# Stationary activation tiles 1088, 1056 and 1040 bytes apart instead of 1024

## The chip, the core and the metric

The kernel runs on one core of one Trainium2 chip. The metric is the device time of one execution in microseconds. Three executions of the kernel before took 1676.47, 1676.90 and 1677.61 us; their median, 1676.9 us, is what the change is measured against.

## What is computed

One decoder layer on 256 tokens with a model width of 2048, all in float32. The parts that matter here are its large matrix products, since nearly all of the time is theirs:

```python
h = _rms_norm(x, attn_norm_g[l])
proj = h @ w_in[l]                      # 2048 x 13312
...
kv = m @ w_mem_kv                       # 2048 x 2048, m is the normalised memory
...
merged = (jax.nn.sigmoid(g_da) * (o_da @ w_o_da[l])
          + jax.nn.sigmoid(g_ret) * (o_ret @ w_o_ret[l])
          + jax.nn.sigmoid(g_mem) * (o_mem @ w_o_mem[l]))
x = x + merged @ w_out[l]
hf = _rms_norm(x, ffn_norm_g[l])
x = x + (jax.nn.silu(hf @ w_ffn_gate[l]) * (hf @ w_ffn_up[l])) @ w_ffn_down[l]   # 2048 x 5632 twice, 5632 x 2048
```

Between them stand a causal differential attention, a chunked retention and a cross-attention into 256 memory tokens, which are small.

## The kernel before

**Operands.** The weights are streamed from HBM in pieces of 256 rows by 512 columns (512 KB each), 584 of them, into a ring of four slots named `raw`. ScalarE copies a piece into `w_hi`, which rounds it to the type float32r (L337, and L374 for the first four), and VectorE writes the rest, `raw - w_hi`, into `w_lo` (L625, L658). The activations are kept transposed, so that they can be the stationary operand: 16 tiles of 128 rows (of the contracted dimension) by 256 tokens, again in a high and a low part. `hT_hi` and `hT_lo` hold the normalised input of the projections, of the gates and of the feed-forward; `oT_hi` and `oT_lo` hold the memory at first, then the outputs of the branches, the merged rows, and the feed-forward's activations. These are the four sets of the title. In each the token is the fastest index, so one tile fills 256 x 4 = 1024 bytes of every partition, and the tiles follow each other without a gap.

**The product.** `three_passes` (L1007) issues three matmuls of 128 x 128 by 128 x 512 for one tile k, one half t of the tokens and one piece: high by high, high by low, low by high. The stationary operand is half a tile, 128 elements or 512 bytes of each partition; the moving operand is one row block of the piece, 512 elements or 2048 bytes of each partition. `pair` (L1014) does that for two tiles and two halves, twelve matmuls on one piece of weights, after a wait on `lo_done`. `chunk_pair` (L1024) puts eight such pairs (four or two where the contracted dimension is shorter) into one accumulation. Each matmul is an instruction for the weight load (named PEld in the profile) and one for the product (PE).

**Order.** Every engine runs a program written out by hand. The slots s of a sweep are the same on all engines: between its pieces TensorE does the small transposes (L1032) and the small products of the attentions (L1070, L1085, L1119 to L1137, L1160 to L1173) in float32. The stages are the memory's key and value, the projections, three gate and branch stages, the output projection, and eleven rounds of the feed-forward, each of 16 pieces of gate and up and 8 of down. In the feed-forward TensorE turns the activations after slot 2, ScalarE and VectorE write the first four tiles of `oT_hi` and `oT_lo` in one instruction each at slot 3 (L585, L957), and TensorE reads them from slot 16 on.

**Memory.** `sb(name, shape, type)` takes the next bytes of each partition. In the order of the calls `raw`, `w_hi` and `w_lo` take 16384 bytes each, then the four sets 16384 bytes each, then `proj` and the rest. Counted from the start of `raw`, the sets begin at 49152, 65536, 81920 and 98304 and `proj` at 114688, all multiples of 1024.

Of the kernel before, what the change touches and what calls it, by code (L numbers as in the profile page):

```python
# [27 lines left out]
F32R = mybir.dt.float32r  # L28
# [5 lines left out]
P = 128  # L34
D = 2048
TB = 2
TOK = TB * P
NCOL = 512
KD = D // P
# [37 lines left out]
def program(nc, x, mem, positions, w_in, da_q_norm_g, da_k_norm_g, da_lambda_q1, da_lambda_k1,  # L77
# [6 lines left out]
    with ExitStack() as ctx:  # L84
        def sb(name, shape, dt=F32):
            return ctx.enter_context(nc.sbuf_tensor(name, shape, dt))
# [5 lines left out]
        raw = sb("raw", [P, RING, 2, NCOL])  # L92
        w_hi = sb("w_hi", [P, RING, 2, NCOL], F32R)
        w_lo = sb("w_lo", [P, RING, 2, NCOL], F32R)
        hT_hi = sb("hT_hi", [P, KD, TOK], F32R)
        hT_lo = sb("hT_lo", [P, KD, TOK], F32R)
        oT_hi = sb("oT_hi", [P, KD, TOK], F32R)
        oT_lo = sb("oT_lo", [P, KD, TOK], F32R)
        proj = sb("proj", [P, TB, GATE0])
        kvm = sb("kvm", [P, TB, D])  # L100
        sq = sb("sq", [P, TB, 2, 256])
# [1177 lines left out]
```

## Time and profile before

| | |
|---|---|
| median of three timed executions | 1676.9 us (1676.47 to 1677.61) |
| span of the profiled execution, first to last instruction | 1674.9 us |
| the median less that span | 2.0 us |
| TensorE products (PE) busy | 1668.0 us, 7592 instructions |
| weight loads (PEld) busy | 1381.3 us, 7592 instructions |
| VectorE (DVE), ScalarE (ACT), GpSimd (POOL) busy | 950.0, 774.7, 31.9 us |
| moved by DMA | 319.96 MB, mean 191 GB/s |

The span is from the trace of one execution; the time of an execution holds about 2 us around it. Matmuls are pipelined: the profile gives each 128 x 512 product about 0.39 us, but one starts every 0.23 us, so that busy time of PE says only that the engine was never empty. What a matmul costs is read from the distance between the starts, or from the length of a stretch of the chain divided by its count. The chain is the sequence of work that ended last, followed back from the end.

### The profile page before, as it was taken

The numbers are of one execution on the slowest core, as the hardware profiler recorded it, in microseconds if no ns is written. First come the engines' busy times: TensorE is split into PE (matmuls) and PEld (weight loads), VectorE is DVE, ScalarE is ACT, GpSimd is POOL, SyncE is SP. The second block draws the span as 40 slices with busy tenths as digits, with TensorE's granted clock in tenths as the row PEclk, the third lists the DMA queues.
The fourth block names the chain that finished last, engine by engine and source line by source line (L and its number), as shares of the span: only waits on it lengthen the run. The fifth ranks groups of instructions, "written<-read, shape, count | busy, mean of one in ns | idle before, by whom it ended". The sixth has DMA issues, their size and how long they took to land.

```text
span 1674.9 us, 21891 instructions
## 1 busy us (share of the span) xinstructions
PE 1668.0 (100%) x7592; PEld 1381.3 (82%) x7592; DVE 950.0 (57%) x1061; ACT 774.7 (46%) x936; POOL 31.9 (2%) x33
## 2 busy tenths in 40 slices
PE   9999999999999999999999999999999999999999
PEld 7888888888888888888888888888888888888887
DVE  5565554454577766655555545565554554655555
ACT  6655454444555544444444544444434444444342
POOL 0000000000111000000000000000000000000000
PEclk9999999999999999999999999999999999999999
DMA  9876555566544565666655666666666666666664
GB/s 340 265 217 187 176 169 168 177 196 192 174 152 150 180 185 175 213 199 190 188 184 184 186 189 192 191 193 188 188 192 190 190 192 188 189 192 191 192 189 151
DMA packets 167095, 319.96 MB, mean 191 GB/s; under 512 B 11152, under 2 KB 15760, under 8 KB 166288
## 3 DMA queue, kind: packets, MB, share of 16 engines
q1 hardware_dynamic: 167056, 319.45, 62.1%
q8 instruction: 24, 0.39, 0.1%
q14 instruction: 15, 0.12, 0.0%
HBM read 317.31 MB, written 2.10 MB: 191 GB/s over the span
## 4 chain that ended last, share of the span: by engine, by line
PE 91%; issue 7%; DVE 1%; DMA 0%; POOL 0%; ACT 0%; DVEq 0%; ACTq 0%; SPq 0%; POOLq 0%
PE acc L1010 87%; PE at L1032 2%; POOL rstd L315 0%; PE at L1070 0%; PE at L1085 0%; DMA raw<-in_w_mem_kv 0%; DVE w_lo L625 0%; DMA raw<-in_w_in 0%; ACT pm L486 0%; PE at L1160 0%; DVE ss L650 0%; ACT w_hi L337 0%; PE at L1172 0%; PE at L1173 0%; PE at L1171 0%
## 5 line engine op out<-in xcount | busy, mean ns | idle before, releaser
L625 DVE TENSOR_TENSOR w_lo<-raw,w_hi 128x1024 fp32r<-128x1024 f32 x580 | 706.7, 1224 | 639.5 <-ACT w_hi L337 637.6
L337 ACT ACTIVATE w_hi<-raw 128x1024 fp32r<-128x1024 f32 x580 | 614.6, 1061 | 829.4 <-PE acc L1010 812.7
L1010 PE MATMUL acc<-w_hi,hT_hi 128*128 128x512 f32 x1568 | 616.7, 393 | 0.0
L1010 PE MATMUL acc<-w_hi,hT_lo 128*128 128x512 f32 x1568 | 611.0, 390 | 0.0
L1010 PE MATMUL acc<-w_lo,hT_hi 128*128 128x512 f32 x1568 | 610.5, 389 | 0.0
L1010 PEld LDWEIGHTS acc<-w_hi,hT_hi 128*128 128x128 f32 x1568 | 294.5, 188 | 62.2 <-issue 1.3
L1010 PEld LDWEIGHTS acc<-w_hi,hT_lo 128*128 128x128 f32 x1568 | 294.4, 188 | 61.9
L1010 PEld LDWEIGHTS acc<-w_lo,hT_hi 128*128 128x128 f32 x1568 | 294.6, 188 | 59.8
L1010 PE MATMUL acc<-w_hi,oT_hi 128*128 128x512 f32 x768 | 300.9, 392 | 1.2 <-DVE oT_lo L644 1.2
L1010 PE MATMUL acc<-w_hi,oT_lo 128*128 128x512 f32 x768 | 299.1, 389 | 0.0
L1010 PE MATMUL acc<-w_lo,oT_hi 128*128 128x512 f32 x768 | 299.0, 389 | 0.0
L1010 PEld LDWEIGHTS acc<-w_hi,oT_hi 128*128 128x128 f32 x768 | 144.2, 188 | 31.4 <-issue 1.6
L1010 PEld LDWEIGHTS acc<-w_hi,oT_lo 128*128 128x128 f32 x768 | 144.2, 188 | 30.1
L1010 PEld LDWEIGHTS acc<-w_lo,oT_hi 128*128 128x128 f32 x768 | 144.3, 188 | 29.4
L927 DVE TENSOR_TENSOR proj<-acc,proj 128x1024 f32<-128x1024 f32 x47 | 57.6, 1225 | 20.6 <-PE acc L1010 20.6
L315 POOL TENSOR_TENSOR rstd<-ms,minus_half 128x4 f32<-128x4 f32 (+1 forms) x16 | 26.9, 1680 | 613.4 <-DVE ms L651 613.4
L365 ACT ACTIVATE proj<-acc,row_rstd 128x512 f32 (+1 forms) x28 | 17.7, 685 | 23.6 <-PE acc L1010 23.6
L951 DVE SCALAR_TENSOR_TENSOR proj<-acc,row_rstd,proj 128x512 f32<-128x512 f32 x22 | 15.5, 747 | 5.9 <-PE acc L1010 5.9
L1032 PEld LDWEIGHTS at<-ident,proj 128*128 128x128 f32 x120 | 14.0, 140 | 2.0
L1032 PE MATMUL at<-ident,proj 128*128 128x128 f32 x120 | 15.5, 272 | 0.0
L650 DVE TENSOR_REDUCE ss<-sq 128x4 f32<-128x512 f32 (+2 forms) x16 | 15.1, 946 | 0.0
L472 ACT ACTIVATE proj<-acc,half_rstd 128x512 f32<-128x512 f32 x24 | 15.1, 681 | 0.0
(151 smaller groups left out, 474.9 us busy)
## 6 DMA issues: line engine op xcount, KB each, us to landing
raw<-in_w_in SPq DMA_DIRECT2D x208, 512.0 KB, 3.9
raw<-in_w_ffn_gate SPq DMA_DIRECT2D x88, 512.0 KB, 3.8
raw<-in_w_ffn_up SPq DMA_DIRECT2D x88, 512.0 KB, 3.7
raw<-in_w_ffn_down SPq DMA_DIRECT2D x88, 512.0 KB, 3.8
raw<-in_w_mem_kv SPq DMA_DIRECT2D x32, 512.0 KB, 6.5
raw<-in_w_out SPq DMA_DIRECT2D x32, 512.0 KB, 3.8
raw<-in_w_o_mem SPq DMA_DIRECT2D x16, 512.0 KB, 5.3
raw<-in_w_o_da SPq DMA_DIRECT2D x16, 512.0 KB, 5.0
```

Of the source, the lines that this page charges most:

```text
L315: nc.gpsimd.tensor_tensor(rstd[:, 0:n], ms[:, 0:n], minus_half[:, 0:n], ALU.pow).then_inc(done, 1)
L337: act.activation(w_hi[:, s % RING], raw[:, s % RING], ACT.Copy).then_inc(hi_done, 1)
L365: e = act.activation(dst[:, t], acc[p][:, t, :], ACT.Copy, scale=row_rstd[:, norm, t:t + 1])
L472: e = act.activation(sg[:, t], acc[0][:, t, :], ACT.Tanh, scale=half_rstd[:, t:t + 1])
L625: v.tensor_tensor(w_lo[:, s % RING], raw[:, s % RING], w_hi[:, s % RING].bitcast(F32), ALU.subtract).then_inc(lo_done, 1)
L650: step(v.tensor_reduce(ss[:, 0:n], src, AX.X, ALU.add), X[summed], i + 1)
L927: v.tensor_tensor(dst, acc[p][:], dst, ALU.add).then_inc(acc_free[p], 1)
L951: e = v.scalar_tensor_tensor(out=gt[:, t], in0=acc[1][:, t, :], scalar=row_rstd[:, 2, t:t + 1], in1=sg[:, t], op0=ALU.mult, op1=ALU.mult)
L1010: e = pe.matmul(acc[p][:, t, :], a[:, k0 + k, tok], w[:, s % RING, k, :], start=first and k == 0 and n == 0, stop=last and k == 1 and n == 2)
L1032: return pe.transpose(out, src, ident[:])
```

## The change

Four lines of the allocation change and two are added. Nothing that an engine computes is changed, no instruction is added or removed, and no wait moves.

```diff
-        hT_hi = sb("hT_hi", [P, KD, TOK], F32R)
-        hT_lo = sb("hT_lo", [P, KD, TOK], F32R)
+        hT_hi = sb("hT_hi", [P, KD, TOK + 16], F32R)[:, :, 0:TOK]
+        hT_lo = sb("hT_lo", [P, KD, TOK + 8], F32R)[:, :, 0:TOK]
         oT_hi = sb("oT_hi", [P, KD, TOK], F32R)
-        oT_lo = sb("oT_lo", [P, KD, TOK], F32R)
+        sb("oT_lo_shift", [P, 32])
+        oT_lo = sb("oT_lo", [P, KD, TOK + 4], F32R)[:, :, 0:TOK]
+        sb("proj_shift", [P, 32])
```

The tiles of `hT_hi`, `hT_lo` and `oT_lo` get 64, 32 and 16 unused bytes behind them, so they lie 1088, 1056 and 1040 bytes apart. `oT_hi` keeps 1024. Two unused pieces of 128 bytes are put ahead of `oT_lo` and of `proj`.

## Rows read from the trace of the kernel before

**Rows 1.** The page: busy time, share and instructions; then tenths by slice.

```profile
PE 1668.0 (100%) x7592; PEld 1381.3 (82%) x7592; DVE 950.0 (57%) x1061; ACT 774.7 (46%) x936; POOL 31.9 (2%) x33
PEclk9999999999999999999999999999999999999999
DMA  9876555566544565666655666666666666666664
```

**Rows 2.** Waits of PE, then of PEld: us in total, times, longest.

```profile
PE at L1032 <- POOL ident L299: 2.0, 1, 2.0
PE acc L1010 <- DVE oT_lo L644: 1.2, 1, 1.2
...
PEld acc L1010 <- issue: 2.9, 5, 1.6
...
PEld acc L1010 <- DVE w_lo L625: 0.7, 3, 0.2
PEld acc L1010 <- DVE w_lo L658: 0.6, 2, 0.3
```

**Rows 3.** Groups of TensorE's large matmuls, by form (PE), then weight loads (PEld).

```profile
L1010 PE MATMUL acc<-w_hi,hT_hi 128*128 128x512 f32 x1568 | 616.7, 393 | 0.0
L1010 PE MATMUL acc<-w_hi,hT_lo 128*128 128x512 f32 x1568 | 611.0, 390 | 0.0
L1010 PE MATMUL acc<-w_lo,hT_hi 128*128 128x512 f32 x1568 | 610.5, 389 | 0.0
L1010 PE MATMUL acc<-w_hi,oT_hi 128*128 128x512 f32 x768 | 300.9, 392 | 1.2 <-DVE oT_lo L644 1.2
L1010 PE MATMUL acc<-w_hi,oT_lo 128*128 128x512 f32 x768 | 299.1, 389 | 0.0
L1010 PE MATMUL acc<-w_lo,oT_hi 128*128 128x512 f32 x768 | 299.0, 389 | 0.0
L1010 PEld LDWEIGHTS acc<-w_hi,hT_lo 128*128 128x128 f32 x1568 | 294.4, 188 | 61.9
```

**Rows 4.** The chain in order of time: start us, us, what and how many.

```profile
8.58 142.13 PE acc L1010 x624
...
199.13 0.87 PE at L1032 x8
...
205.48 1.73 PE at L1070 x8
...
712.77 108.84 PE acc L1010 x480
...
1061.97 65.33 PE acc L1010 x288
1128.17 65.30 PE acc L1010 x288
```

**Rows 5.** The small products at L1070 by form: PE, then PEld.

```profile
L1070 PE MATMUL at<-sq 128*128 128x256 f32 x32 | 7.5, 379 | 0.0
L1070 PEld LDWEIGHTS at<-sq 128*128 128x128 f32 x32 | 6.1, 189 | 0.9
```

**Rows 6.** Timeline of PE where `hT` gives way to `oT`: start, length.

```profile
1427.69 0.39 PE L1010 MATMUL acc<-w_lo,hT_hi 128*128 128x512 f32 x1
1427.92 0.39 PE L1010 MATMUL acc<-w_hi,hT_lo 128*128 128x512 f32 x1
1428.15 0.39 PE L1010 MATMUL acc<-w_hi,oT_hi 128*128 128x512 f32 x1
...
1439.93 0.39 PE L1010 MATMUL acc<-w_lo,oT_hi 128*128 128x512 f32 x1
```

**Rows 7.** Window of one feed-forward round: length, busy PE, PEld, DVE, ACT, POOL, clock, DMA.

```profile
1061.97:1128.17 66.20, 66.20 (x297) 54.90 (x297) 36.39 (x31) 27.53 (x28) 0.00 (x0) 1.00 0.63 190
```

**Rows 8.** The lines that write four tiles at once: ns min/median/max, starts.

```profile
L585 ACT ACTIVATE oT_hi<-at x10: 1008/1011/1012, 995.9 to 1591.7; 128x1024 fp32r<-128x1024 f32 x10
...
L957 DVE TENSOR_TENSOR oT_lo<-at,oT_hi x10: 1217/1218/1219, 997.2 to 1592.9; 128x1024 fp32r<-128x1024 f32 x10
```

**Rows 9.** Timeline of PE just behind eight transposes.

```profile
199.75 0.47 PE L1010 MATMUL acc<-w_hi,hT_hi 128*128 128x512 f32 x1
200.07 0.39 PE L1010 MATMUL acc<-w_lo,hT_hi 128*128 128x512 f32 x1
200.30 0.40 PE L1010 MATMUL acc<-w_hi,hT_lo 128*128 128x512 f32 x1
200.53 0.40 PE L1010 MATMUL acc<-w_hi,hT_hi 128*128 128x512 f32 x1
...
202.38 0.39 PE L1010 MATMUL acc<-w_hi,hT_lo 128*128 128x512 f32 x1
```

## The prediction

> **What bounds the kernel.** I read the page's busy times first, then the waits of TensorE, then the chain in order of time, and last the timeline of single matmuls. The page says that the products fill the whole span and that the clock is at its upper level, 2.4 GHz, in every slice [rows 1]. The waits say that almost nothing holds TensorE up: the entries of its large matmuls come to 1.2 us on the product side and 4.2 us on the weight-load side, together 5.4 us of 1674.9 [rows 2]. VectorE and ScalarE are busy half the time and wait for TensorE; DMA has a third of its time left. So the end is set by the number of matmuls times the distance between their starts. The kernel has 3 x 1568 + 3 x 768 = 7008 large ones [rows 3]. A round of the feed-forward shows the distance: 288 of them in 65.30 to 65.33 us, which is 226.7 ns each; a stretch of 480 in the middle gives 108.84 / 480 = 226.8 ns; even the first 624, behind cold buffers and with DMA nearly full, give 227.8 ns [rows 1, 4]. 7008 x 226.7 ns = 1588.7 us, 95% of the span. The other 86 us are 8.6 us before the first large matmul and the 584 small ones with the steps into and out of them. Only what changes the 226.7 ns can matter.
>
> **What the change does, step by step.** No instruction, wait or DMA is added, removed or moved, so the sum has one term that can be other than zero: 7008 matmuls by the change of their distance. To see which matmuls get another address I count by tile. `hT_hi` is stationary in 3136 of them, `hT_lo` in 1568, `oT_lo` in 768 and `oT_hi` in 1536 [rows 3]. Counted from the start of `raw`, the sets now begin at 49152, 66560, 83456 and 99968, and `proj` at 116736, still a multiple of 1024 like all that lies behind it. Before, each stationary half tile began on a multiple of 512 bytes. Now `oT_hi` still does; `hT_hi` does for tiles 0 and 8, `hT_lo` for tile 0, `oT_lo` for none, as its start is 128 bytes past such a multiple. A tile of `hT_lo` is used 96 times (48 sweeps, two halves), tiles 0 to 3 eight times more in the last stage, and one of `hT_hi` twice as often. That leaves 2736 + 1464 + 768 = 4968 matmuls with a stationary operand that begins elsewhere than on a multiple of 512. All of them begin on a multiple of 16.
>
> *The weight load.* It is contiguous, 128 elements, before and after, and the profile gives it 188 ns [rows 3]. It runs beside the product ahead of it, and the next product starts 226.7 ns after that one, so 39 ns of it are spare: a load that took a fifth longer would still be hidden. I cost it at nothing; without that cover every added ns would count 4968 times, 5 us for each.
>
> *The distance.* Here the trace of before has no operand that lies off a multiple of 512 bytes, so I bound the cost from both sides with the nearest rows. The small float32 products at L1070 have the same weight load, 189 ns, and take 1.73 / 8 = 216.2 ns each in the chain [rows 4, 5]. At 2.4 GHz that is 519 cycles, and 226.7 ns are 544. A record there moves 256 columns, and half the number of columns in nearly the same time says that each is passed twice. So a float32r matmul that moves 512 columns once is 10.5 ns dearer than a float32 record that moves 256 twice. The two differ in how fast the moving operand is read. The 10.5 ns are therefore either a fixed charge of the float32r form, or what a weight load and a moving stream at twice the rate cost each other in the memory. Only the second can depend on where the tiles lie, and it gives the bounds: at best the 10.5 ns go away in all 4968 matmuls, -52 us; at worst they are paid a second time, +52 us.
>
> I take zero, and these rows decide it. If the place of the stationary operand relative to the moving one mattered, the distance would vary already: the weights go round in four slots of 4096 bytes with two halves of 2048, the tiles step by 1024 and 512, so that their distance takes many values, and yet tile after tile and set after set keep the distance. From 1428.15 to 1439.93 there are 52 starts in 11.78 us, 226.5 ns each, all with `oT`, whose set lies 32768 bytes behind the other [rows 6]. VectorE and ScalarE reach into the same memory for 36.4 and 27.5 of the 66.2 us of a round, DMA engines for 63% [rows 7], and no stretch of the timeline shows a matmul pushed aside by them; a memory in which accesses collide by address should show such jitter. What these rows can't exclude is an effect of address bits below 512, since no operand has used them.
>
> The Trainium skill (TensorE: Matmul & The Clock Gate, What happens when you issue a matmul) says that loading the next tile's weights takes no read bandwidth from the running matmul, since each has a read port of its own. By that the address is of no account and the sum is zero too. The same page (Back-to-back issue gap) gives about 215.8 ns for 512 columns at 2.4 GHz, which the float32 row of this trace supports (216.2) and its float32r rows don't (226.7); it does not say what the difference is, and by its gap the kernel would stand 7008 x 10.9 ns = 76 us lower, an estimate from that page.
>
> *The writers.* The instructions that fill one tile at a time keep their form. Those that write four tiles in one go (L585 and L957, eleven each in all) now write four runs of 1024 bytes with gaps, where that set is padded [rows 8]. Even at twice 1.22 us such an instruction would be hidden: it comes at slot 3 of a round and its tiles are read from slot 16 on, 13 pieces x 12 x 226.7 ns = 35 us later. Its cost is nothing; if that cover were gone it would be at most 11 x 1.22 = 13 us.
>
> **Sum.** 1674.9 us of the profiled execution plus 0, and 2.0 us around it: 1676.9 us, the median of before. About 0.2%, 3.4 us, is what a measurement of this kernel can tell from no change; that is 0.48 ns per large matmul, or 0.68 ns for each of the 4968.
>
> **Rivals.**
> 1. *Faster: the shift breaks up a collision.* The 10.5 ns would be lost because weight load and moving stream, both starting on a multiple of 512, run over the same low address bits together; a stationary operand that starts 16, 32 or 64 bytes further on would slip between. For it speaks that the float32 rows lack the 10.5 ns [rows 4, 5] and that the distance isn't wholly rigid: behind eight transposes ten starts run from 200.07 to 202.38 in 2.31 us, 231 ns each, before they settle [rows 9]. Against it speaks that the settled value is the same for every tile and slot. All shifted matmuls: -52 us, 1624.7. If only one in four falls well: 1242 x 10.5 ns = -13 us, 1663.9.
> 2. *Slower: the weight load is fetched in larger pieces.* If the 10.5 ns are what fetching 512 bytes in aligned pieces takes from the moving stream, a tile that straddles needs one piece more. With pieces of 64 bytes that is 1/8 more, 1.3 ns, for the 784 + 576 = 1360 matmuls of `hT_lo` and `oT_lo` off such a multiple: +1.8 us, not measurable. With 128 bytes it is 2.6 ns for 1568 + 1176 + 632 = 3376: +8.9 us, 1685.8. With 256 bytes 5.25 ns for 4464: +23 us, 1700.3. It decides from pieces of 128 bytes up. For it speaks that a shifted start has never been tried here; against it that the same cost must first be one of fetching, and not a fixed one.
> 3. *The writers show.* A late `oT_lo` would hold TensorE at slot 16 of each round. At most 13 us, 1690; the 35 us of cover speak against it, and the list of waits has no entry of that kind.
>
> **How the numbers follow.** No change: 0.68. Faster by a collision that goes: 0.17, spread between -4 and -52 us with more weight on the small end, as the tiles now fall on many offsets and few need fall well. Slower by straddled pieces: 0.13, most of it at 9 us. The writers: 0.02. The likeliest case gives 1676.9 us, and by itself 1674 to 1680. The range goes on to 1663 and 1688 to take in the quarter of rival 1 and the 128-byte case of rival 2, which brings what is left out to about 2 in 10. Faster 0.17, same 0.68, slower 0.15.
>
> **What would show it.** A round of the feed-forward (288 matmuls) should again take 65.3 us in the chain and the weight loads 188 ns. Rival 1 or 2 would show as a distance that depends on the tile: with `hT_hi` tiles 0 and 8 as before and the others not, and with `oT_hi` as a control in every pair. The down product of a round, which uses `oT_hi` twice and `oT_lo` once, would then move less than gate and up. Rival 3 would show as a wait of PEld for L957. I would be wrong if the low address bits of a stationary operand matter to a float32r stream, of which no row of before can tell.

## The result: 1.6% slower

The changed kernel takes 1704.66 us (median) where the kernel before takes 1677.0 us in the same comparison: a ratio of 1.0163, 95% interval 1.0147 to 1.018. The forecast was no change, 1676.9 us, with a range up to 1688, so the time lies outside the range. Its side, slower, had been given 0.15. One of the four executions of the changed kernel took 9690.84 us, as one of ten with the sets 256 bytes on (below) took 6063.19, and both are left out of the comparisons.

The page of the changed kernel shows the same picture as [rows 1], only longer. (In it all line numbers are two higher.)

```profile
span 1702.9 us, 21898 instructions
PE 1694.8 (100%) x7592; PEld 1383.7 (81%) x7592; DVE 950.7 (56%) x1061; ACT 774.7 (45%) x936; POOL 28.8 (2%) x33
PEclk9999999999999999999999999999999999999999
```

The number of instructions of each engine is equal and the clock stays at its upper level. VectorE and ScalarE are as busy as before to within 0.7 us. TensorE's weight loads still wait for next to nothing (us in total, times, longest):

```profile
PEld acc L1012 <- issue: 3.3, 5, 2.0
...
PEld acc L1012 <- DVE w_lo L660: 1.3, 2, 1.1
```

So no wait has appeared; the large matmuls have moved apart. The chain in order of time shows it, against [rows 4]; the first stretch has 624 matmuls here too, but the chain enters it at the thirteenth, so its times are not to be compared with those of before:

```profile
12.06 141.58 PE acc L1012 x612
...
723.02 110.96 PE acc L1012 x480
...
1078.28 66.58 PE acc L1012 x288
...
1145.73 66.60 PE acc L1012 x288
```

A stretch of 480 takes 110.96 instead of 108.84 us, one of 288 takes 66.60 instead of 65.30: 231.2 ns per matmul instead of 226.7. The distances between successive large matmuls, added up over the whole trace (without the ones that span small products or waits, over 245 ns), are 1556.4 us before and 1585.4 us after: 29.0 us more, against 28.0 us of span. So the result is all in these distances.

Two groups say what it is not. By form, the weight load of a padded set takes what it took [rows 3]. And the products on `oT_hi`, whose tiles did not get another pitch, are longer too (392 ns each before), so that it is not only the padded tiles that pay:

```profile
L1012 PEld LDWEIGHTS acc<-w_hi,hT_lo 128*128 128x128 f32 x1568 | 295.3, 188 | 69.7
```
```profile
L1012 PE MATMUL acc<-w_hi,oT_hi 128*128 128x512 f32 x768 | 303.2, 395 | 2.5 <-DVE oT_lo L646 1.8 <-DVE w_lo L660 0.7
```

The timeline of the same kernel shows the new rhythm. Its distances are no longer 0.227 us throughout but run from 0.22 to 0.24, and the trace has the same sequence in each of nine rounds (place by place, the standard deviation from round to round is 0.6 ns in the mean):

```profile
1083.66 0.41 PE L1012 MATMUL acc<-w_hi,hT_hi 128*128 128x512 f32 x1
1083.90 0.40 PE L1012 MATMUL acc<-w_lo,hT_hi 128*128 128x512 f32 x1
1084.13 0.39 PE L1012 MATMUL acc<-w_hi,hT_lo 128*128 128x512 f32 x1
1084.36 0.39 PE L1012 MATMUL acc<-w_hi,hT_hi 128*128 128x512 f32 x1
...
1085.74 0.39 PE L1012 MATMUL acc<-w_hi,hT_hi 128*128 128x512 f32 x1
1085.96 0.39 PE L1012 MATMUL acc<-w_lo,hT_hi 128*128 128x512 f32 x1
```

A sequence that repeats so closely points to the addresses, which repeat too, and not to chance encounters with other engines; it does not prove it. The open questions were whether each misplaced tile pays for itself or disturbs the others, whether pitch, start or distance from the moving operand counts, and whether the other engines have a part.

### The profile page after: what moved, and what is told of

Same layout as the page of the kernel before. It is cut to its first block, busy times and chain, and to the rows that moved or that the text cites. A ratio compares the mean times of both kernels' runs of the same rounds, so it can differ in the third digit from the quotient of the medians.

```text
span 1702.9 us, 21898 instructions
## 1 busy us (share of the span) xinstructions
PE 1694.8 (100%) x7592; PEld 1383.7 (81%) x7592; DVE 950.7 (56%) x1061; ACT 774.7 (45%) x936; POOL 28.8 (2%) x33
## 4 chain that ended last, share of the span: by engine, by line
PE 99%; DMA 0%; DVE 0%; SPq 0%; ACT 0%; issue 0%
PE acc L1012 95%; PE at L1034 2%; DMA raw<-in_w_mem_kv 0%; PE at L1072 0%; PE at L1087 0%; PE at L1123 0%; PE at L1121 0%; PE at L1162 0%; PE at L1138 0%; PE at L1174 0%; PE at L1175 0%; PE at L1139 0%; PE at L1173 0%; PE at L1137 0%; DVE w_lo L660 0%; ACT w_hi L376 0%
## 5 line engine op out<-in xcount | busy, mean ns | idle before, releaser
L1012 PE MATMUL acc<-w_hi,hT_hi 128*128 128x512 f32 x1568 | 625.6, 399 | 0.0
L1012 PE MATMUL acc<-w_lo,hT_hi 128*128 128x512 f32 x1568 | 617.4, 394 | 0.0
```

The lines of the kernel that those rows point to most:

```text
L1012: e = pe.matmul(acc[p][:, t, :], a[:, k0 + k, tok], w[:, s % RING, k, :], start=first and k == 0 and n == 0, stop=last and k == 1 and n == 2)
```

## Experiments

### One padded set at a time

```diff
# e1_hT_hi_only
-        hT_hi = sb("hT_hi", [P, KD, TOK], F32R)
+        hT_hi = sb("hT_hi", [P, KD, TOK + 16], F32R)[:, :, 0:TOK]
# e2_hT_lo_only (the fill of 512 bytes brings the next set back to a multiple of 1024)
-        hT_lo = sb("hT_lo", [P, KD, TOK], F32R)
+        hT_lo = sb("hT_lo", [P, KD, TOK + 8], F32R)[:, :, 0:TOK]
+        sb("hT_lo_fill", [P, 128])
# e3_oT_lo_only
-        oT_lo = sb("oT_lo", [P, KD, TOK], F32R)
+        oT_lo = sb("oT_lo", [P, KD, TOK + 4], F32R)[:, :, 0:TOK]
+        sb("oT_lo_fill", [P, 192])
```

> Only hT_hi is padded (1088 bytes); every other tensor begins on a multiple of 1024 as before. Changed kernel: +27.7 us for 4968 shifted matmuls, 5.6 ns each. Theory P (each shifted stationary tile pays for itself): 2736 shifted matmuls, +15 us, 1692. Theory S (one misplaced set disturbs the rhythm of all matmuls in its stages, the aligned ones too): all 4704 matmuls of the hT stages at about 231 ns, +20 us or more, 1697. Theory B (the cost comes from where the sets begin, 128 or 512 bytes on, and not from the pitch): 1677.

> Only hT_lo is padded (1056 bytes). Theory P: 1464 shifted matmuls, +8 us, 1685. Theory S: the same as with hT_hi alone, +20 us, 1697. Theory B: 1677.

> Only oT_lo is padded (1040 bytes), beginning on a multiple of 1024 as before. Theory P: 656 matmuls with tiles off a multiple of 512, +3.7 us, 1680.7. Theory S: all 2304 matmuls of the oT stages at 230 to 231 ns, +8 us, 1685. Theory B: 1677.

Measured, against 1676.19 us for the kernel before in the same comparison:

| kernel | median us | change | ratio (95% interval) |
|---|---|---|---|
| hT_hi alone | 1695.12 | +18.9 | 1.0115 (1.0098 to 1.0132) |
| hT_lo alone | 1698.43 | +22.2 | 1.0132 (1.0115 to 1.0149) |
| oT_lo alone | 1682.47 | +6.3 | 1.0037 (1.0023 to 1.0051) |

`hT_lo` is the stationary operand of half as many matmuls as `hT_hi` and costs more, so that one price for every misplaced tile is ruled out. The three add up to 47.4 us where the change as a whole costs 27.7, and the first two alone to 41.1, though their tiles have the same remainders modulo 256 bytes as in the change (the probes below show that these are what counts). So no tile simply pays a price of its own. Theory B falls too, since these kernels keep the start of every set on a multiple of 1024. In the stages of the padded set most matmuls are late, whichever set they read. With `hT_hi` alone padded, a stretch of 480 on `hT` takes 231.3 ns each, the level of the changed kernel:

```profile
322.98 111.04 PE acc L1010 x480
```

With `oT_lo` alone padded the time, 1682.47 us, lies between the 1680.7 of theory P and the 1685 of theory S and decides nothing. Its trace does: in the stages on `oT` the distance from one matmul on the unmoved `oT_hi` to the next on `oT_hi` is 229.7 ns in the mean, where the kernel with `hT_hi` alone padded has 227.1.

### TensorE alone

A kernel of nothing but matmuls, in the order of `three_passes`, with the offsets as parameters (in float32 elements). It and the two probes below ran once each; their aligned stages agree with each other, 226.7 ns where the clock is at its upper level and no misplaced stage stands just ahead, and so do their stages with both sets 64 bytes on, 233.3.

```python
def addresses(n, h, l, p_h, p_l, m_h, m_l):
    for s in range(8 * n):
        for k in range(2):
            for t in range(2):
                tile = 2 * (s % 8) + k
                hi = h + tile * (256 + p_h) + 128 * t
                lo = l + tile * (256 + p_l) + 128 * t
                w = (s % 4) * 1024 + k * 512
                yield s // 8 % 2, t, st_hi[:, hi:hi + 128], mv_hi[:, m_h + w:m_h + w + 512]
                yield s // 8 % 2, t, st_hi[:, hi:hi + 128], mv_lo[:, m_l + w:m_l + w + 512]
                yield s // 8 % 2, t, st_lo[:, lo:lo + 128], mv_hi[:, m_h + w:m_h + w + 512]
...
for i, (b, t, a, w) in enumerate(addresses(2, 0, 0, 16, 0, 0, 0)):      # high tiles 1088 bytes apart
    e = pe.matmul(acc[b][:, t, :], a, w, start=i % 96 in (0, 3), stop=i % 96 in (92, 95))
```

> A kernel of TensorE alone: 25 stages of 192 float32r matmuls (128x128 by 128x512) in the order of the layer kernel's three passes, no waits between them, other engines idle; its output is the input x, the layer is not computed. The stages differ only in where the stationary and the moving operands begin. Theory P (the place of each stationary tile has a price of its own): the aligned stages take 226.7 ns per matmul, 43.5 us; a stage with one padded set is dearer in proportion to the matmuls on that set, about 5.6 ns for each shifted one, so high at 1088 about +3.7 ns in the mean and low at 1056 about +1.8; both sets moved by one common offset cost as much as both padded. Theory R (it is the offset between weight load and moving stream, or between one stationary tile and the next): moving all operands by 64 bytes costs nothing, and a common start offset of both stationary sets costs either nothing or the same as the padding. Theory E (the other engines' accesses are needed for the loss): no stage differs from the aligned one by more than 0.5 ns.

Each stage has a line of its own, so the chain of this kernel lists them (start us, us, what and how many):

```profile
73.33 44.40 PE acc L78 x192
117.73 44.57 PE acc L82 x192
162.30 44.21 PE acc L86 x192
206.51 44.45 PE acc L90 x192
250.97 43.55 PE acc L94 x192
...
427.66 43.52 PE acc L110 x192
...
514.71 44.62 PE acc L118 x192
...
648.92 44.80 PE acc L130 x192
693.72 44.62 PE acc L134 x192
738.33 43.52 PE acc L138 x192
...
914.96 43.96 PE acc L154 x192
...
1002.49 44.80 PE acc L162 x192
1047.29 43.55 PE acc L166 x192
```

| line | what is moved | ns per matmul |
|---|---|---|
| L94 | nothing | 226.8 |
| L78 | high tiles 1088 apart | 231.3 |
| L82 | low tiles 1056 apart | 232.1 |
| L86 | low tiles 1040 apart | 230.3 |
| L90 | high 1088, low 1056, as in the change | 231.5 |
| L110 | all tiles 1280 apart | 226.7 |
| L118 | both sets begin 4 on, pitch 1024 | 232.4 |
| L130 | both sets begin 64 on | 233.3 |
| L134 | both sets begin 128 on | 232.4 |
| L138 | both sets begin 256 on | 226.7 |
| L154 | only the moving operands begin 64 on | 229.0 |
| L162 | only the high moving operand begins 64 on | 233.3 |
| L166 | stationary and moving operands all begin 64 on | 226.8 |

Theory E falls: with the other engines idle the loss is the same. Theory P falls: one set moved costs as much as both. Theory R holds. A pitch of 1280 costs nothing, a start 64 bytes on costs the full amount without any change of pitch, and moving everything by 64 costs nothing. What counts, in all these stages, is the distance in bytes between the stationary and the moving operand, modulo 256. It is not a sum over single matmuls, though: with only the high moving operand 64 on (L162) a third of the matmuls keep their distance, and yet the stage is slower than with both moved (L154).

### The same in the layer kernel

```diff
# e4_all_by_64: everything that TensorE reads goes 64 bytes on
+        sb("ring_shift", [P, 16])
         w_hi = sb("w_hi", [P, RING, 2, NCOL], F32R)
# e5_sets_by_64: the stationary sets and all behind them; [P, 64] is e6_sets_by_256, [P, 4] is e8_sets_by_16
+        sb("sets_shift", [P, 16])
         hT_hi = sb("hT_hi", [P, KD, TOK], F32R)
```

> The kernel before with 64 unused bytes ahead of w_hi: w_hi, w_lo, all four stationary sets and everything behind them begin 64 bytes on; raw stays. Theory R (the distance between stationary and moving operand): nothing changes, 1676.2 to 1677. Theory A (the operands' own alignment to 256 or 512 bytes): all 7008 matmuls pay about 6 ns, +42 us, 1718.

> The kernel before with 64 unused bytes ahead of hT_hi: the four stationary sets and everything behind them begin 64 bytes on, their tiles stay 1024 apart; w_hi and w_lo stay. Theory R: all 7008 matmuls at 233.4 ns instead of 226.7, +47 us, 1723, more than the padding cost although no pitch is changed. Theory T (the changing offset from tile to tile is what disturbs): no change, 1676.5.

> As the kernel with 64 unused bytes ahead of hT_hi, but 256 bytes. Theory R, modulo 256: 1676.5. If the period is 512 or more in the kernel: up to 1723.

| kernel | median us | before us | ratio (95% interval) |
|---|---|---|---|
| all by 64 | 1677.38 | 1677.5 | 1.0 (0.999 to 1.0009) |
| sets by 64 | 1719.08 | 1677.5 | 1.0248 (1.0231 to 1.0266) |
| sets by 256 | 1676.97 | 1677.5 | 0.9997 (0.9987 to 1.0007) |

Theories A and T fall. One unused piece of 64 bytes, with every tile still 1024 bytes from the next, costs 41.6 us, one and a half times what the padding cost; if the moving operands go along it costs nothing. The chain of the kernel with the sets 64 bytes on gives 67.20 / 288 = 233.3 ns, the value of L130 above:

```profile
1086.97 67.20 PE acc L1011 x288
...
1155.04 67.20 PE acc L1011 x288
```

With the sets 256 bytes on, and with all 64 on, the same stretches are back at 65.30 and 65.33 us.

The expectation said +47 us, 5 us too much. Of the distances in its trace up to 245 ns the sum is 1599.9 us, 43.5 more than before, while 7008 x 6.6 ns would be 46 us. One part of this is that not every large matmul has a large one next to it; another that before, 395 distances were already 229 ns or more, 381 of them within twelve matmuls behind a small product, such as those in [rows 9].

### Pitch without a change of distance, and the filler alone

```diff
# e7_interleaved
-        hT_hi = sb("hT_hi", [P, KD, TOK], F32R)
-        hT_lo = sb("hT_lo", [P, KD, TOK], F32R)
+        hT = sb("hT", [P, KD, 2, TOK], F32R)
+        hT_hi, hT_lo = hT[:, :, 0, :], hT[:, :, 1, :]
# e9_fillers_only
+        sb("oT_lo_shift", [P, 32])
         oT_lo = sb("oT_lo", [P, KD, TOK], F32R)
+        sb("proj_shift", [P, 224])
```

> hT_hi and hT_lo share one tensor, high and low tiles in turn: the tiles of each lie 2048 bytes apart, all begin on a multiple of 1024. Theory R: the pitch itself is of no account, 1677. If a pitch other than 1024 costs: up to 1700.

> Of the change only the filler ahead of oT_lo: oT_lo begins 128 bytes on, all pitches 1024, proj and the rest on a multiple of 1024. Theory P (each misplaced stationary tile pays 5.6 ns): 768 matmuls, +4 us, 1681. Theory S (all 2304 matmuls of the oT stages pay, some 3 to 6.6 ns as in the probe's stages with one set moved): +7 to +15 us, 1684 to 1692.

With a pitch of 2048 the time is 1677.26 against 1677.56 us, ratio 0.9999 (0.999 to 1.0009): the pitch by itself is of no account here. With `oT_lo` 128 bytes on and nothing else it is 1684.87 us, +7.3, ratio 1.0044 (1.0028 to 1.0061). So the filler that the change puts ahead of `oT_lo` costs something without any padding, and its 768 matmuls cannot carry that at 5.6 ns each. The trace has the distances in the stages on `oT` as 227, 232 and 234 ns in turn (means): the one ahead of the matmul on `oT_lo` and the one behind it are long, the one between the two on `oT_hi` is not.

```profile
1047.45 0.39 PE L1012 MATMUL acc<-w_hi,oT_hi 128*128 128x512 f32 x1
1047.67 0.40 PE L1012 MATMUL acc<-w_lo,oT_hi 128*128 128x512 f32 x1
1047.90 0.40 PE L1012 MATMUL acc<-w_hi,oT_lo 128*128 128x512 f32 x1
1048.14 0.39 PE L1012 MATMUL acc<-w_hi,oT_hi 128*128 128x512 f32 x1
```

So even here, where only one matmul in three is misplaced, two distances in three are long.

### How offsets, operand widths and types enter

> Again TensorE alone, without waits, output the input x: 18 stages of 192 float32r matmuls with both stationary sets begun c bytes on (c = 16 to 240 in steps of 16, and 8, 248, 252), pitch 1024, moving operand unmoved, and then, at c = 0 and 64, stages of 96 with 64 or 32 stationary columns, with 256 moving columns, in float32 and in bfloat16. In the first probe c = 0 and 256 gave 226.7 ns, c = 16, 32, 64 gave 233.3, 128 gave 232.3, and the moving operand 64 on (c = -64) 229.0. Theory R (only the distance of the stationary operand from the moving one matters, modulo 256): c = 192 gives 229.0, and the price runs through intermediate values in between; c = 0 is the cheapest of all. Theory M (some distance is better than zero, as the 10.5 ns over the float32 products may be a collision at c = 0 too): at least one c gives less than 226.7, at best 216. Theory F (the loss goes with the amount fetched for the stationary operand): with 64 and 32 columns the excess over 216 ns at c = 0 falls to a half and a quarter. Float32, with half the moving rate, and bfloat16, with half the bytes, should not care for c.

| both sets begin c bytes on | ns per matmul |
|---|---|
| c = 0, 16, 240, 252 | 226.7 to 226.8 |
| c = 192 | 228.9 |
| c = 176, 8, 80 | 230.0, 230.7, 232.0 |
| c = 32, 48, 64, 112, 128, 144, 160, 208, 224, 248 | 233.3 to 233.4 |
| c = 96 | 234.3 |

(c = 0 by its second half, since the clock was at its lower level in the first.) c = 192 gives what moving the moving operand by 64 gave, as theory R asks, -64 and 192 being the same modulo 256. But c = 16 gave 226.7 here and 233.3 in the first probe, where it stood behind another misplaced stage, and c = 128 gave 233.3 here and 232.4 there. And four bytes cost nothing on one side (c = 252) but 5.7 ns on the other (232.4 with both sets 4 bytes on, L118). No c gave less than 226.7 ns; theory M found nothing. The later stages in the chain (96 large matmuls each, 192 records in float32):

```profile
883.46 22.08 PE acc L170 x96
905.54 22.24 PE acc L174 x96
927.78 11.52 PE acc L178 x96
939.30 41.44 PE acc L182 x192
980.79 10.74 PE acc L186 x49
...
1046.05 11.31 PE acc L198 x96
1057.36 41.44 PE acc L202 x192
1098.85 10.74 PE acc L206 x49
```

L170 and L174 have 64 and 32 stationary columns at c = 0: 230.0 and 231.7 ns, more than with 128, not less. Theory F falls, and with it rival 2 of the prediction as it was put, a cost in proportion to what is fetched. Float32 (L182 at c = 0, L202 at c = 64) takes 41.44 / 192 = 215.8 ns at either offset, and bfloat16 (L186, L206) shows distances of 216 ns at either (the 10.74 us of 49 records are 48 distances and the length of the last product). Of the three types only float32r is sensitive. It is the one that moves four bytes per column in a single pass, if float32 passes its columns twice as the prediction reads it; that this is the reason is not shown.

### What one misplaced operand does

The same probe with one operand in 24 moved, and with stages entered from an aligned or from a misplaced one:

```python
def nudged(every, st, mv, n=1):
    ...
    hit = m % every == every // 2       # m counts the matmuls
    a = (2 * (s % 8) + k) * 256 + 128 * t + (st if hit else 0)
    w = (s % 4) * 1024 + k * 512 + (mv if hit else 0)
```

> TensorE alone again, output the input x, aligned stages of 96 matmuls between the others. (a) One operand in 24 is moved by 64, 16, 128 or 256 bytes, or one moving operand in 24 by 64. Theory P (a price for each misplaced load): the loss stays in one or two intervals, at most 7 ns per event, 0.3 ns in the mean. Theory S (the misplaced operand knocks the pair of streams out of a rhythm that takes several matmuls to settle): 5 to 15 intervals are longer than 227, in sum 20 to 50 ns per event. 256 bytes: nothing under both. (b) Always the same stationary and moving operand: S and R give 226.7 with both at the same offset and 233.3 with the stationary one 64 on, so that no change of address is needed. (c) Both sets begun 16, 240 or 252 bytes on, once behind an aligned stage and once behind a stage at +64: if what counts is the rhythm in which a stage is entered, these offsets keep 226.7 in the first case and 233.3 in the second; if it is the offset alone, both cases agree.

One stationary operand moved by 64, in the timeline (each row's start less the one before is a distance):

```profile
92.98 0.39 PE L119 MATMUL acc<-mv_hi,st_hi 128*128 128x512 f32 x1
...
95.25 0.39 PE L119 MATMUL acc<-mv_lo,st_hi 128*128 128x512 f32 x1
95.48 0.39 PE L119 MATMUL acc<-mv_hi,st_lo 128*128 128x512 f32 x1
95.70 0.40 PE L119 MATMUL acc<-mv_hi,st_hi 128*128 128x512 f32 x1
95.94 0.39 PE L119 MATMUL acc<-mv_lo,st_hi 128*128 128x512 f32 x1
96.17 0.40 PE L119 MATMUL acc<-mv_hi,st_lo 128*128 128x512 f32 x1
96.40 0.39 PE L119 MATMUL acc<-mv_hi,st_hi 128*128 128x512 f32 x1
```

From 92.98 to 95.25 ten matmuls start 227 ns apart, and so does the next. The matmul at 95.70 has the misplaced operand. From 95.48 on the trace has distances of 226, 235, 229, 232 and 231 ns, and after that 227 again. All eight events of the stage go this way: 20 ns lost per event, in four distances, three of which lie between matmuls with aligned operands. A stationary operand 128 bytes on costs 13 to 14 ns, in two distances (233, 234); a moving operand 64 bytes on 46 to 47 ns, over eight; 16 and 256 bytes cost nothing. That is theory S in kind. In size it expected 5 to 15 long distances and 20 to 50 ns per event: the moving operand fits that, the stationary one spreads less at 64 bytes, and at 128 it stays below in both.

The second part, from the chain of the same kernel:

```profile
409.27 21.76 PE acc L159 x96
431.03 22.40 PE acc L163 x96
...
475.21 43.52 PE acc L171 x192
...
541.14 44.80 PE acc L179 x192
...
673.64 43.84 PE acc L195 x192
...
805.17 44.80 PE acc L211 x192
```

L159 and L163 use one and the same stationary and moving operand throughout: 226.7 ns with both at the same offset, 233.3 with the stationary one 64 on. So no address need ever change for the loss to appear. L171 and L179 are the same stage, both sets 16 bytes on: 226.7 ns behind an aligned stage, 233.3 behind one at 64. Likewise 240 bytes gave 226.7 and then 228.3 (L195), 252 bytes 226.7 and then 233.3 (L211). At these offsets two rhythms hold, and what went before decides. It is not decided by the level of the stage ahead alone: in the second probe 240 and 252 bytes stood behind stages at 233.3 ns and yet settled at 226.7. Which rhythm the layer kernel falls into was tried with its sets 16 bytes on:

> 16 unused bytes ahead of hT_hi: all four stationary sets begin 16 bytes on, pitch 1024. The probes gave 226.7 ns behind an aligned stage and 233.3 behind a misplaced one. If the offset alone counts it is 1677 or 1723. If the rhythm counts: the layer kernel breaks it with transposes 80 times, and the time is between, or at 1723 if these throw it into the slower one.

It takes 1719.09 against 1677.56 us, ratio 1.0248 (1.023 to 1.0265), with 288 matmuls in 67.19 us, 233.3 ns: the slower one, in all but 34 of its 6853 distances up to 245 ns.

## Why the prediction was wrong

**What bounds the kernel** was right: 7008 large matmuls times their distance, and the sum had one term that could be other than zero. No wait appeared and the writers stayed hidden.

**The weight load** was read rightly as 188 ns with cover, 188 ns after too. But the end of a load is not the only way in which it meets the product beside it.

**The distance** is the step that failed: "I take zero, and these rows decide it". They did not. That the distance is equal for many tiles and ring slots [rows 6] was taken as a sign that place is of no account. All those places are multiples of 512 apart, and the period found is 256, so by this measure they are one and the same place; the text itself said that no operand had used the bits below 512, and then gave that gap too little weight. The second argument, that a memory with collisions would show jitter under the load of VectorE, ScalarE and DMA [rows 7], looked at the wrong parties: the effect needs TensorE alone. In place of zero the runs showed 226.7 ns when the stationary and the moving operand lie a multiple of 256 bytes apart and 233.3 ns at most other distances (234.3 at 96 bytes); the changed kernel, in which some tiles still fall on such a multiple, has 231.2. Counted by the period of 256, it has 4464 misplaced matmuls (the count in rival 2) and not 4968.

**The bound** was about right and should have shaped the range: at worst +10.5 ns per shifted matmul, 52 us. The worst measured in the layer kernel is 6.6 ns per matmul, with all 7008 misplaced, 41.6 us. In the changed kernel the loss, 27.7 us, falls on misplaced and aligned matmuls alike, 4.0 ns per matmul in the mean over all 7008.

**The rules of the Trainium skill.** TensorE: Matmul & The Clock Gate (What happens when you issue a matmul) has the next weight load take no read bandwidth from the running matmul, as each has its own port. What the prediction drew from it, that the address is of no account, does not hold for float32r in these traces: the same stage goes from 226.7 to 233.3 ns with the stationary operand's place. Whether read bandwidth is what it loses, no run shows. The page's gap for 512 columns (Back-to-back issue gap, about 215.8 ns) is met by bfloat16 (216) and by the float32 records of 256 columns (215.8), and never by float32r.

**Rival 1** (faster) fell: of some twenty offsets none gave less than 226.7 ns. Its evidence was misread. The ten distances of 231 ns behind eight transposes [rows 9] were no sign that the 10.5 ns could go away. They end in 236, 229, 232, 231 and then 227 ns, nearly as the probe has it behind a single misplaced operand, so the trace of before held the same kind of disturbance; that the transposes cause it in the same way is inferred.

**Rival 2** had the right side, and its case of 256 bytes the time 1700.3, close to 1704.7. That is luck, as the mechanism was wrong: operands that straddle such pieces cost nothing if the moving ones are shifted too, a narrower stationary operand costs more instead of less, and aligned matmuls pay as well.

**Rival 3** did not occur: no load waits for L959, the former L957. Of the signs that the prediction named, the weight loads stayed at 188 ns, a round took 66.6 instead of 65.3 us, and in the feed-forward the matmuls of the down product moved less than those on `hT`, by 3.8 against 4.7 ns in the mean.

**What stays open.** The runs show on what the loss depends, not which part of the memory or of TensorE makes it. A weight load runs beside the product ahead of it, and nothing here tells apart whether the distance to that product's moving operand counts or to its own's, since in nearly all stages the moving operands lie on one offset. That both operands are read in pieces that get into each other's way is argued only. Open are also why 10.9 ns over the float32 distance remain at the best offset, why single offsets such as 80, 176 and 192 cost less than their neighbours, and what sets the rhythm in which a stage at 16, 240 or 252 bytes settles.

## What to carry to other kernels

Where float32r matmuls follow each other at their full rate, put stationary and moving operands on the same offset modulo 256 bytes, and if tiles are padded or fillers put between tensors, use multiples of 256. A tensor put ahead of the operands for another reason can cost 2.5% with no instruction changed, as its 64 bytes did here. And rows that agree over many cases exclude an effect only for the cases that they hold: here they all shared the one property that the change gave up.

## What the runs showed of the hardware that was not expected

- A float32r matmul of 128 x 128 by 128 x 512 starts every 226.7 ns at best, and every 233.3 ns where stationary and moving operand are off by 32 to 160 bytes modulo 256 (232.0 at 80, 232.4 once at 128, 234.3 at 96), and also at 208, 224 and 248. Float32 and bfloat16, at 216 ns, gave the same at 0 and at 64.
- One misplaced stationary operand (64 or 128 bytes) costs 13 to 20 ns and one misplaced moving operand (64 bytes) 46 ns, spread over two to eight distances around and behind it.
- At offsets of 16, 240 and 252 bytes two rhythms hold, 226.7 and 228.3 or 233.3 ns, and what ran before decides between them.
- With 64 or 32 stationary columns instead of 128 the aligned float32r matmul gets slower, 230.0 and 231.7 ns. With 256 moving columns the aligned stage takes 11.52 us for 96 and the one 64 bytes off 11.31: there alone the misplaced operand was the cheaper one (one stage each).
